# Output projection banks moved ahead of one head pair's scores, and one step of probabilities moved ahead of low parts

## The reference, cut to what matters

```python
proj = rms_norm(x, ln1) @ w_in             # split into queries, keys, values, gates
y_moba  = moba_attention(mq, mk, mv)       # 6 heads of 64; one block of 256 keys: causal softmax attention
y_mlstm = rms_norm(mlstm_chunkwise(...) * sigmoid(xo))   # 4 heads
y_swa   = swa_attention(sq, sk, sv, sinks) # 6 query heads on 2 key heads, window of 128, with a sink
x = x + concatenate([y_moba, y_mlstm, y_swa]) @ w_out    # 1024 x 1024
u = rms_norm(x, ln2) @ w_up
x = x + square(relu(u)) @ w_down
```

## Time and profile before

| | us |
|---|---|
| three timed runs | 1399.66, 1400.93, 1402.45 |
| their median | 1400.93 |
| the profiled execution, its own time | 1398.38 |
| its span, first to last instruction | 1396.6 |
| mean granted TensorE clock | 0.997 of full speed |
| VectorE busy | 1137.2 (81%) |
| ScalarE busy | 850.2 (61%) |

### The profile page before, as it was taken

The page is one execution under the profiler, slowest core; times in us unless marked ns, Lnnn a source line. Parts: engine busy times, 40 slices in busy tenths (PEclk is TensorE's granted clock), DMA queues, the critical chain, the costliest instruction groups (busy, mean ns, idle before and its releaser), DMA issues.

```text
span 1396.6 us, 25742 instructions
## 1 busy us (share of the span) xinstructions
PE 1376.9 (99%) x10381; PEld 1296.5 (93%) x10381; DVE 1137.2 (81%) x1706; ACT 850.2 (61%) x1315; POOL 101.3 (7%) x157
## 2 busy tenths in 40 slices
PE   8999999999999999999999999999999999999998
PEld 7898888899888888899999999998899999999987
DVE  7898998868898998767787789988778877877653
ACT  6776776435876875446577484553565774755452
POOL 2000111000000011003100001111031000000000
PEclk9999999999999999999999999999999999999999
DMA  9643999866446999769945679999599556878662
GB/s 270 160 144 101 287 274 269 254 170 181 136 135 181 292 269 278 221 189 276 286 143 167 188 228 288 308 295 284 168 261 311 153 154 183 237 216 235 184 186 72
DMA packets 472982, 301.34 MB, mean 216 GB/s; under 512 B 15116, under 2 KB 454416, under 8 KB 472736
## 3 DMA queue, kind: packets, MB, share of 16 engines
q1 hardware_dynamic: 455344, 239.57, 61.5%
q0 software_dynamic: 16704, 58.29, 12.7%
q10 hardware_dynamic: 816, 1.84, 0.4%
HBM read 289.43 MB, written 1.05 MB: 208 GB/s over the span
## 4 chain that ended last, share of the span: by engine, by line
PE 90%; DVE 5%; ACT 2%; issue 2%; DMA 1%; SPq 0%; ACTq 0%; DVEq 0%
PE acc L2136 14%; PE acc L2137 14%; PE acc L2138 14%; PE mx L2153 12%; PE mx L2154 7%; PE acc L2153 6%; PE acc L2154 3%; PE mx L2136 2%; PE mx L2137 2%; PE mx L2138 2%; DVE w_lo L1184 1%; PE acc L2181 1%; DMA raw<-in_w_in 1%; PE acc L2183 1%; PE acc L2182 1%
## 5 line engine op out<-in xcount | busy, mean ns | idle before, releaser
L1184 DVE TENSOR_TENSOR w_lo<-raw,w_hi 128x1024 fp32r<-128x1024 f32 x450 | 542.2, 1220 | 106.9 <-ACT w_hi L593 104.6
L593 ACT ACTIVATE w_hi<-raw 128x1024 fp32r<-128x1024 f32 x450 | 466.3, 1053 | 159.3 <-DMA raw<-in_w_in 62.2
L2136 PE MATMUL acc<-h,w_hi 128*128 128x256 f32 (+1 forms) x1472 | 418.7, 284 | 5.7 <-DVE h L1211 3.4
L2137 PE MATMUL acc<-h,w_hi 128*128 128x256 f32 (+1 forms) x1472 | 412.8, 280 | 0.0
L2138 PE MATMUL acc<-h,w_lo 128*128 128x256 f32 (+1 forms) x1472 | 411.6, 280 | 0.0
L2136 PEld LDWEIGHTS acc<-h,w_hi 128*128 128x128 f32 x1472 | 277.3, 188 | 10.9 <-DVE h L1211 3.9
L2137 PEld LDWEIGHTS acc<-h,w_hi 128*128 128x128 f32 x1472 | 277.5, 189 | 1.4 <-issue 1.0
L2138 PEld LDWEIGHTS acc<-h,w_lo 128*128 128x128 f32 x1472 | 277.9, 189 | 0.0
L2153 PE MATMUL mx<-u,w_hi 128*128 128x512 f32 x756 | 263.0, 391 | 0.0
L2154 PE MATMUL mx<-u,w_lo 128*128 128x256 f32 x756 | 213.1, 282 | 0.0
L2153 PEld LDWEIGHTS mx<-u,w_hi 128*128 128x128 f32 x756 | 141.9, 188 | 29.5
(11 more groups left out here) (341 smaller groups left out, 2288.5 us busy)
## 6 DMA issues: line engine op xcount, KB each, us to landing
raw<-in_w_in SPq DMA_DIRECT2D x132, 512.0 KB, 4.3
ada<-in_w_ada POOLq DMA_DIRECT2D x96, 512.0 KB, 5.9
raw<-in_w_ffn_in SPq DMA_DIRECT2D x88, 512.0 KB, 4.5
raw<-in_w_up SPq DMA_DIRECT2D x64, 512.0 KB, 5.6
raw<-in_w_down SPq DMA_DIRECT2D x64, 512.0 KB, 4.7
raw<-in_w_out SPq DMA_DIRECT2D x32, 512.0 KB, 3.9
raw<-in_w_ffn_out SPq DMA_DIRECT2D x32, 512.0 KB, 4.4
raw<-in_w_ret_o SPq DMA_DIRECT2D x16, 512.0 KB, 4.0
```

The costliest lines, as they stand in the source:

```text
L593: nc.scalar.activation(w_hi[:, n % NS], raw[:, n % NS], ACT.Copy).then_inc(hi_ready, 1)
L1184: V.tensor_tensor(w_lo[:, n % NS], raw[:, n % NS], w_hi[:, n % NS].bitcast(F32), ALU.subtract).then_inc(lo_ready, 1)
L2136: mm(outp, w_hi[:, i % NS, k], rhs[:, k, 0], start=k == 0, stop=False)
L2137: mm(outp, w_hi[:, i % NS, k], rhs[:, k, 1], start=False, stop=False)
```

## The change

On TensorE, banks (2,3) and (3,2) of the output projection, which stood behind the scores of pair 4 and the outputs of pair 2, are put ahead of both, directly after the transposes of pair 2. On VectorE, `probabilities(5)`, which stood behind low parts 28, 29 and 30, is put behind 28 and ahead of 29 and 30. Both hold for the two layers of the first block.

```diff
                 probabilities(4)
                 maxima(5)
                 outputs(3)
+                lo_upto(p0 + 28)
+                probabilities(5)
                 lo_upto(p0 + 30)
-                probabilities(5)
                 outputs(4)
                 lo_upto(p0 + 32)
                 outputs(5)
@@
                 out_bank(2, 2)
                 pe.wait_ge(at_y, l * 6 + 2)
                 turn(2)
+                out_bank(2, 3)
+                out_bank(3, 2)
                 pe.wait_ge(at_e, l * 6 + 4)
                 at_scores(4)
                 at_outputs(2)
-                out_bank(2, 3)
-                out_bank(3, 2)
                 out_bank(3, 0)
                 out_bank(3, 1)
                 pe.wait_ge(at_y, l * 6 + 3)
```

## The result

The changed kernel takes 1406.38 us (median of 10 runs, 1403.79 to 1408.66); the kernel before, in runs beside it, 1399.89 us (10 runs, 1399.09 to 1404.21). The ratio is 1.0042 (95% interval 1.0032 to 1.0051), which is 5.9 us slower (4.5 to 7.1). Forecast were 5.1 us and 1406.0. The profiled execution took 1405.49 us, its span is 7.1 us longer than before.

A forecast was written before the change was run, and what follows sets the result against it. TensorE is 99% busy, but VectorE's chain is the tight one in the stretch. Per layer 2.02 + 0.53 = 2.55 us, 5.1 us in two, on the median 1400.93 gives 1406.0 us; range 1402.2 to 1409.0.

The forecast's parts named there:

- The place and the releaser: After pair 2's transposes: bank (2,3) runs directly, bank (3,2) waits for slab 3's low part, scores follow without gap.
- TensorE's waits: Changed stretch: about 1.7 us before bank (3,2), 1.2 before pair 3's transposes, 0.7 among the later standstills.
- VectorE passes it on: VectorE waits for the late scores, starts the maxima 2.02 us late and keeps that lateness to the last transposes.
- maxima 2.0 us after the end of that low part's slot: Sign on VectorE: the maxima follow the end of slab 3's low part by 2.0 us and not 0.3.
- The second part: VectorE's tail: probabilities moved ahead of low parts 29 and 30 wait for exponentials, adding 0.53 us per layer.
- The sum: Last transposes come 2.02 + 0.53 = 2.55 us late per layer, 5.1 us in two layers.
- no later slack swallows the loss: Between the last transposes and layer 1's same place, the longest TensorE wait is 0.2 us, so no delay vanishes.
- Only the second part: Rival: slab 3's low part is not late; last transposes 0.73 us late, 1.5 us in all, 1402.4; chance 0.10.
- the gap is simply filled: Rival: TensorE does 1.05 us of work in its old gap per layer, 2.1 us gained, 1398.8; chance 0.06.
- The clock's fall: Rival: TensorE's clock falls once per layer behind the new waits, 3.4 us on top, 1409.4; chance 0.08.
- fourth rotation: VectorE's rotation of keys and queries before the fifth pair's scores, last step 112.44 to 113.13, which the scores need.
- a fixed shift: Layer 1 was said to repeat layer 0's stretch 0.81 us off a fixed shift, with 300.8 us between rows.

The follow-up runs named there:

- Experiment 1: Kernel before with only the first part, banks (2,3) and (3,2) ahead of the fifth pair's scores, VectorE's order old: ratio 1.0021, +2.9 us.
- experiment 3: Kernel before with only bank (2,3) ahead of the fifth pair's scores, bank (3,2) and VectorE's order as before: ratio 0.9997, -0.4 us.
- experiment 7: Changed kernel with the outputs of pair 4 ahead of low part 30 instead of behind it: ratio 1.0039, +5.5 us against the kernel before.
- experiment 9: Kernel before with the first part (both banks) alone, run again on the same chip as the changed kernel: ratio 1.0028, +3.9 us.
- experiment 4: Kernel before with ready banks (2,2) and (2,3) between pair 2's transposes and the fifth pair's scores, (3,2) staying behind: ratio 0.9994, -0.8 us.
- experiment 5: Kernel before with both banks moved and slab 3's low part made before the rotation instead of after it: ratio 1.0014, 2.0 us.

## Why the prediction was right

- **The place and the releaser** held: bank (2,3) in the old gap, bank (3,2) waiting for the low part, the scores directly behind it, no wait for the rotation. The low part started at 113.95 and the bank 1.28 later, the 1.28 that the earlier trace rows gave.
- **TensorE's waits** were put at 1.7, 1.2 and 0.7 us and are 1.56, 0.98 and 0.49 in the profile's count, which takes the modelled end of the matmul before; the starts are as forecast, within 0.1 us of their distance to the rotation.
- **VectorE passes it on.** The maxima were to come 2.02 us late. Counted from the rotation's last step they start at 117.45 - 113.22 = 4.23 where it was 114.73 - 112.44 = 2.29, so 1.94 late. The 0.08 lies between masks and maxima: 1.50 us before, when TensorE came out of a wait, 1.41 now (117.45 - 116.04), when it comes from a bank. The sign "maxima 2.0 us after the end of that low part's slot" did not fit the prediction's own sum, which has 2.35 (116.75 - 114.40); the hole is 2.27. Experiment 1 gives 1.95 for the whole first part.
- **The second part** was put at 0.53 and is 0.51 alone, 0.53 on top of the first (2.48 - 1.95). Its hole is 0.44 on VectorE as counted from the low part's listed end; a next instruction that is ready starts 0.09 before that end (the three low parts are 3.50 long and the next starts 3.41 behind their start).
- **The sum** was 2.55 per layer and is 2.48: 5.0 us in all where 5.1 were forecast. The timed 5.9 (4.5 to 7.1) and 5.5 (3.6 to 7.4) hold both. That the time itself was met within 0.4 us (1406.0 and 1406.38) is partly luck: the forecast stands on a median of 1400.93 from three runs, ten runs of the same kernel have 1399.89, and the timed difference came out larger than the sum by about as much. That no later slack swallows the loss held as well: a matmul that stood at 642.67 comes at 648.44 in the changed kernel, 5.77 late, which is the 0.78 from ahead of the stretch and 4.99.
- **The rivals.** "Only the second part" falls with experiment 1, "the gap is simply filled" with experiment 3, where 0.62 of its 1.05 us were filled and nothing was won. The clock's fall is half true: it happened in one pass, layer 0 of the changed kernel's second profile. The new wait of 1.56 us occurs in ten profiled passes (the changed kernel's two profiles, experiments 1, 7 and 9), and in the other nine the granted clock stayed at 1.00 in the 7 to 10 us around it. But its price was set too high. The term was 1.7 us for a fall; it cost 0.36 (18.25 - 17.89), which is what the slower scores held VectorE up, since TensorE had a wait of 0.98 us to lose the rest in. With that price it adds less than a timed comparison shows, so the rival's 1409.4 is not what a fall in this place gives. The argument against the rival was weak: that the first matmul after the wait of 1.77 us took only 0.38 us shows nothing, because it also took 0.38 at the same place of the changed kernel's first profile, and there the clock fell a microsecond later.
- **Two slips of reading** in the prediction carry nothing. Its "fourth rotation" is `rope(4)`, the fifth. And layer 1 is not off a fixed shift: 300.8 us lie between the layers in both pairs of rows.

What only the trace carries is the second part's loss and the gain of the earlier half; the timed runs do not exclude zero for either.

## What to carry to other kernels

A gap of the busiest engine is not worth its length when another engine's written-out chain sets the pace: filling it moved the wait 5 us down the line, and the stretch became 0.02 us shorter. Before a piece of work is pulled ahead of the step that feeds the tight engine, look up when the piece's own input is made; a 0.7 us piece whose input came late cost 2 us per layer. And of an instruction with two inputs, find out which one is late before moving the other ahead. And a difference of a few microseconds between two profiled executions is not yet an effect: read it from distances within the stretch that was changed.

## What the runs showed of the hardware

The same kernel with the same wait (1.56 us of TensorE idle, at 113.2 to 114.8 and 113.7 to 115.2 us) had its granted clock fall to 0.50 in one execution, more than 1 us after the wait had ended, and not in the other. The twelve output matmuls of pair 2 that follow then took 1.55 us instead of 0.88. The Trainium skill, TensorE: Matmul & The Clock Gate, section "What's actually happening", lets the clock fall when TensorE has recently been idle; this case's traces agree in one pass of ten (0.50 over 117 to 119 us) and show that the wait alone does not decide it. The start of the program says the same: all twelve profiles have a wait of 1.5 to 2.1 us for a low part there, and behind it the clock fell in one (0.66 over 12 to 17 us, after a wait of 1.94 us) and stayed at 1.00 in the eleven others, one with a wait of 2.05 us among them. What else decides stays open.

The lower level also costs different executions different amounts. Behind the waits of about 2.2 and 1.2 us near 1005 us the clock fell in all twelve profiles, but its mean over 1000 to 1020 us was 0.91 in five of them (the kernel before, the changed kernel's two, experiments 4 and 5) and 0.83 in the other seven. From the matmul behind the first of these waits to the end of the span it was 392.2 to 394.0 us in the five and 393.1 to 395.9 in the seven.
